# Paired attentions: ScalarE copies both heads' transposes in one instruction, reciprocals for two steps at a time, scores four steps ahead

## The chip, the cores and the metric

The kernel runs on one core of a Trainium2 chip. The metric is the device time of one execution in microseconds (us). The program fills and empties itself within that time: all inputs come from HBM and the result is written back there.

## What is computed

Two networks, one behind the other, on 512 tokens of 1024 features, all in float32. The first has two layers: feed-forward, mixer, feed-forward. The mixer of layer 0 (the "even" one) runs a sparse attention (8 heads in a compressed, a selected and a windowed branch, mixed by gates) beside a dilated attention of 8 heads. The mixer of layer 1 is a multi-head attention with latent projections (MLA) of 16 heads. The second network has a pooling layer and an attention layer with conditioning and convolutional feed-forwards.

```python
def first_block(x, ...):
    for l in range(DEPTH):                      # DEPTH = 2
        x = x + 0.5 * _swiglu(_rms_norm(x, ffn1_norm[l]), ...)
        h = _rms_norm(x, mix_norm[l])
        if l % 2 == 0:
            x = x + _even_mixer(h, ...)
        else:
            x = x + _mla_mixer(h, ...)
        x = x + 0.5 * _swiglu(_rms_norm(x, ffn2_norm[l]), ...)
    return _rms_norm(x, final_norm)

def _probs(scores, mask):
    s = jnp.where(mask, scores.astype(jnp.float32), -MASK_BIG)
    m = jnp.max(s, axis=-1, keepdims=True)
    p = jnp.where(mask, jnp.exp(s - m), 0.0)
    l = jnp.sum(p, axis=-1, keepdims=True)
    l_safe = jnp.where(l > 0, l, 1.0)
    return p / l_safe, (m + jnp.log(l_safe))[..., 0]
```

All that matters here is the causal attention with a softmax: for each head, scores q k^T with a mask, exponentials less the row's maximum, division by the row's sum, and the product with v.

## The kernel before

The kernel is one program written out by engine: each engine has its own instruction stream, and semaphores order them. A weight matrix comes from HBM in tiles (`w_raw`), ScalarE and VectorE split each into a high and a low part (`w_hi`, `w_lo`, lines 1863 and 1883), and TensorE multiplies in three passes (lines 1022 to 1024). That is most of the kernel's time.

The change touches the "paired attention", which is used twice: in the even mixer for 12 pairs of heads (`even_phase`: 8 with gates, being four pairs of heads in two branches, then 4 dilated ones), and in the MLA mixer for 8 pairs. A pair `u` has two heads `a` = 0, 1 and four steps `c` = 0 to 3, one for each block of 128 queries; step `t` = 4u + c. A step with index c covers (c + 1) x 128 keys, since the attention is causal. The eight PSUM banks are used so (`at.bank`): 0 to 3 for scores, two for each parity of t; 4 and 5 for the transposes of head 0 and head 1; 6 and 7 for outputs. One step passes these stations:

- `scores(t)` on TensorE (line 1149): both heads' scores into two banks. In the even mixer three passes (lines 1165, 1167, 1169), in MLA one float32 product (line 1172). It waits until the maxima of t - 2 have freed the banks.
- `maxima(t)` on VectorE (line 2720): adds the mask, writes scores to `wk.sm` in SBUF (shown as scores_even, scores_mla) and takes the row's extreme; one instruction for each head, each followed by a read of the accumulator.
- `exps(t)` on ScalarE (line 2014): exponentials in place, with the row sums in `L`; one for each head.
- `inverse(t)` and `share(t)` on VectorE (lines 2729, 2739, 2741): the reciprocal of both heads' sums, then the scaling of the probabilities, with the gate in the same instruction where there is one.
- `turn_(t)` on TensorE (line 1182): c + 1 transposes of 128 x 128 for each head, head 0 into bank 4, head 1 into bank 5.
- `take(t)`: ScalarE copies head 0's transposes from bank 4 to `wk.pT` (line 2022), VectorE copies head 1's from bank 5 (line 2749). Shown as probs_T_even, probs_T_mla.
- `values(t)` on TensorE (line 1200): the product with v, accumulated in an output bank. After the last step of an output ScalarE and VectorE split the bank into a high and a low part (lines 2032, 2759).

Each engine runs a loop over t with a fixed order. TensorE, after scores 0 to 2: turn_(t), side work, scores(t + 3), values(t - 1). ScalarE, after exps 0 to 2: take(t), exps(t + 3), output, side work. VectorE: take(t), maxima(t + 3), inverse(t + 2), share(t + 2), output, side work. The side work (`beside`, `later`, `added`; lines 1399 to 1402 and 618) exists in the even mixer only: in steps 0 to 5 transposes of values and of compressed probabilities, which ScalarE copies out (lines 1309, 1389, 2078, 2131); splits of queries and keys at steps 5, 8, 11 and so on (lines 1961, 2623); the compressed branch's values after steps 7, 15, 23, 31 (line 1396). Behind the loop follows the output projection (`project_out`, line 1022), whose first weight tiles are loaded and split before it or during it.

## Time and profile before

| | us |
|---|---|
| median of 3 runs | 3224.36 (3220.76 to 3226.31) |
| the profiled execution | 3229.91 |
| its span, first to last instruction | 3228.1 |
| TensorE (PE) busy | 3151.1 (98%) |
| VectorE (DVE) busy | 2001.4 (62%) |
| ScalarE (ACT) busy | 1251.4 (39%) |
| GpSimd (POOL) busy | 179.7 (6%) |
| mean granted TensorE clock | 0.986 of full |

The granted clock is a share of TensorE's upper level, 2.4 GHz; the lower level, 1.2 GHz, is 0.5, and a mean between them is a stretch with both. Busy time of TensorE is partly modelled: the ends of pipelined matmuls overlap the starts of the next, so a stretch in which TensorE waits can look fuller than it is. An instruction's start to the next one's start on the same engine is a better measure of what it costs than its duration, since durations overlap. The chain that ended last is followed back from the end of the program, at each step to what released it.

### The profile page before, as it was taken

Reading aid. Unit: us, or ns where it says so; the run is one execution under the profiler, and the core shown is the slowest. Engines: PE = TensorE matmul, PEld = TensorE weight load, DVE = VectorE, ACT = ScalarE, POOL = GpSimd, SP = SyncE. Lnnn points to the kernel's source line nnn. Section 1 sums busy time; section 2 is a strip of 40 time slices with the busy share of each in tenths; the row PEclk is TensorE's granted clock in tenths of the full one; section 3 lists DMA queues with packets and bytes.
Section 4 is the critical chain, followed back from the end, with each engine's and each line's share of the span. In section 5 each row is a group of like instructions: output and inputs, shape, how many; then the busy total and the mean of one; then the engine's idle time right before and its main releaser. Section 6 shows DMA issues by size and latency. Waiting matters only on the chain.

```text
span 3228.1 us, 43254 instructions
## 1 busy us (share of the span) xinstructions
PE 3151.1 (98%) x15791; PEld 2606.1 (81%) x15791; DVE 2001.4 (62%) x2858; ACT 1251.4 (39%) x1940; POOL 179.7 (6%) x176
## 2 busy tenths in 40 slices
PE   8999999899999999999999999999999999989999
PEld 6888877678888888886688888989888887878887
DVE  6764557966654676457775554997555465565543
ACT  3222423643222422236542233765334343443332
POOL 1000011100000000000020000432000001000000
PEclk9999998999999999999999999999999998999999
DMA  6542342015533455222145433544333230123322
GB/s 182 171 139 100 108 117 65 1 55 165 171 115 100 124 163 149 98 97 66 47 130 172 134 100 109 164 150 144 92 103 98 85 101 4 32 74 91 104 98 72
DMA packets 388600, 346.12 MB, mean 107 GB/s; under 512 B 12512, under 2 KB 340637, under 8 KB 388477
## 3 DMA queue, kind: packets, MB, share of 16 engines
q1 hardware_dynamic: 388477, 344.49, 35.5%
q8 instruction: 76, 1.25, 0.2%
q14 instruction: 47, 0.39, 0.0%
HBM read 338.22 MB, written 2.10 MB: 105 GB/s over the span
## 4 chain that ended last, share of the span: by engine, by line
PE 86%; DVE 9%; ACT 2%; issue 1%; SPq 1%; DMA 0%; POOL 0%; ACTq 0%; DVEq 0%; POOLq 0%
PE ps L1022 26%; PE ps L1023 26%; PE ps L1024 26%; DVE w_lo L1883 2%; PE ps L1112 1%; PE ps L1172 1%; PE ps L1182 1%; PE ps L1200 1%; DVE scores_even L2720 1%; SPq L913 1%; PE ps L1101 1%; ACT scores_even L2014 1%; PE ps L1744 0%; PE ps L1745 0%; PE ps L1743 0%
## 5 line engine op out<-in xcount | busy, mean ns | idle before, releaser
L1022 PE MATMUL ps<-a_hi,w_hi 128*128 128x512 f32 (+1 forms) x2920 | 1105.4, 379 | 31.0 <-DVE t L3249 10.9
L1023 PE MATMUL ps<-a_lo,w_hi 128*128 128x512 f32 (+1 forms) x2920 | 1098.8, 376 | 0.0
L1024 PE MATMUL ps<-a_hi,w_lo 128*128 128x512 f32 (+1 forms) x2920 | 1098.6, 376 | 0.0
L1883 DVE TENSOR_TENSOR w_lo<-w_raw,w_hi 128x1024 fp32r<-128x1024 f32 (+1 forms) x526 | 642.4, 1245 | 173.8 <-ACT w_hi L1863 170.9
L1863 ACT ACTIVATE w_hi<-w_raw 128x1024 fp32r<-128x1024 f32 (+1 forms) x526 | 543.5, 1046 | 353.7 <-PE ps L1024 294.3
L1022 PEld LDWEIGHTS ps<-a_hi,w_hi 128*128 128x128 f32 x2920 | 551.6, 189 | 139.2 <-issue 29.2
L1023 PEld LDWEIGHTS ps<-a_lo,w_hi 128*128 128x128 f32 x2920 | 551.7, 189 | 101.1 <-issue 2.0
L1024 PEld LDWEIGHTS ps<-a_hi,w_lo 128*128 128x128 f32 x2920 | 551.4, 189 | 100.4
L1022 PE MATMUL ps<-hs_hi,w_hi 128*128 128x512 f32 x1008 | 392.7, 390 | 1.0 <-DVE hs_lo L3216 1.0
L1024 PE MATMUL ps<-hs_hi,w_lo 128*128 128x512 f32 x1008 | 392.2, 389 | 0.0
L1023 PE MATMUL ps<-hs_lo,w_hi 128*128 128x512 f32 x1008 | 392.1, 389 | 0.0
L2345 ACT ACTIVATE t<-t 128x512 f32<-128x512 f32 x88 | 55.6, 632 | 518.0 <-DVE t L3193 518.0
L3195 DVE TENSOR_TENSOR t<-ps,rstd 128x512 f32<-128x512 f32 x88 | 60.8, 691 | 294.7 <-PE ps L1024 294.7
L2359 ACT ACTIVATE hs_hi<-hid 128x512 fp32r (+1 forms) x126 | 79.5, 631 | 406.0 <-PE ps L1024 406.0
L1022 PEld LDWEIGHTS ps<-hs_hi,w_hi 128*128 128x128 f32 x1008 | 189.2, 188 | 40.9 <-DVE hs_lo L3216 1.5
L1024 PEld LDWEIGHTS ps<-hs_hi,w_lo 128*128 128x128 f32 x1008 | 189.2, 188 | 39.3
L1023 PEld LDWEIGHTS ps<-hs_lo,w_hi 128*128 128x128 f32 x1008 | 189.2, 188 | 38.9
L3216 DVE TENSOR_TENSOR hs_lo<-hid,hs_hi 128x512 fp32r<-128x512 f32 x106 | 73.3, 691 | 218.3 <-ACT hs_hi L2359 218.3
L3181 DVE SCALAR_TENSOR_TENSOR t<-ps,cols,t 128x511 f32<-128x511 f32 x88 | 66.0, 750 | 188.4 <-ACT t L2338 188.4
L3238 DVE SCALAR_TENSOR_TENSOR ada_acc<-ada_raw,cond,ada_acc 128x1024 f32<-128x1024 f32 x147 | 180.5, 1279 | 0.0
L2338 ACT ACTIVATE t<-ps,cols 128x512 f32<-128x512 f32 x88 | 68.5, 779 | 206.7 <-PE ps L1024 206.7
L3208 DVE TENSOR_TENSOR hid<-t,t 128x512 f32 x108 | 74.8, 693 | 16.9 <-DVE t L3195 8.7
(384 smaller groups left out, 3168.3 us busy)
## 6 DMA issues: line engine op xcount, KB each, us to landing
w_raw<-in_ffn_w_up SPq DMA_DIRECT2D x220, 512.0 KB, 4.7
w_raw<-in_ffn_w_down SPq DMA_DIRECT2D x154, 512.0 KB, 3.5
ada_raw<-in_ada_w SPq DMA_DIRECT2D x96, 512.0 KB, 3.9
w_raw<-in_ffn_w_gate SPq DMA_DIRECT2D x88, 512.0 KB, 5.0
w_raw<-in_ev_w_in SPq DMA_DIRECT2D x20, 512.0 KB, 4.3
w_raw<-in_attn_w_qkv SPq DMA_DIRECT2D x12, 512.0 KB, 3.6
w_raw<-in_mla_w_out SPq DMA_DIRECT2D x8, 512.0 KB, 3.6
w_raw<-in_attn_w_o SPq DMA_DIRECT2D x8, 512.0 KB, 3.6
```

What stands on the lines that cost most here:

```text
L1022: mm(dst, hi, rhi, start=start, stop=False)
L1023: mm(dst, hi, rlo, start=False, stop=False)
L1024: return mm(dst, lo, rhi, start=False, stop=stop)
L1863: nc.scalar.activation(w_hi[:, s, 0:width], w_raw[:, s, 0:width], ACT.Copy).then_inc(hi_made.sem, 1)
L1883: nc.vector.tensor_tensor(w_lo[:, s, 0:width], w_raw[:, s, 0:width], w_hi[:, s, 0:width].bitcast(F32), ALU.subtract).then_inc(lo_made.sem, 1)
L2338: do(t[:, 0:T], ps[:, ph.half + 2 * (f % 2) + side, 0:T], ACT.Identity, scale=conv_column(1, side, f, it), bias=conv_column(3, side, f, it ...
L2359: do(dst, src, ACT.Copy).then_inc(h_hi_s.sem, 1)
L3181: v.scalar_tensor_tensor(t[:, 1:T], src[:, 0:T - 1], conv_column(0, side, f, it), t[:, 1:T], ALU.mult, ALU.add).then_inc(mid.sem, 1)
L3195: v.tensor_tensor(t2[:, 0:T], ps[:, f2 + 1, 0:T], rstd[:, 0:T], ALU.mult).then_inc(up_s.sem, 1)
L3208: v.tensor_tensor(hid[:, bass.ds(it * 2 + f, 1), 0:T], t1[:, 0:T].unsqueeze(1), t2[:, 0:T].unsqueeze(1), ALU.mult).then_inc(h_s.sem, 1)
L3216: v.tensor_tensor(lo, src, hi.bitcast(F32), ALU.subtract).then_inc(h_lo_s.sem, 1)
L3238: last = v.scalar_tensor_tensor(acc, ada_raw[:, u, :], cond[:, c, bass.ds(it, 1)], acc, ALU.mult, ALU.add)
```

## The change

It touches the paired attentions alone.

- The copies. For steps with c = 0, 1 and 2 ScalarE copies both heads' transposes in one instruction, and VectorE has no copy; for c = 3 both copy one head each, as before. Both heads' transposes lie side by side in one bank for c = 0 (bank 4, 256 columns) and c = 1 (bank 5, 512 columns); for c = 2 they lie in banks 4 and 5, and ScalarE's instruction reads 384 columns of each; the new `place(t, a)` says where. ScalarE's copy now waits for both heads' transposes where c < 3.
- TensorE's waits follow from that: `turn_` waits for ScalarE's copy of the step before (c = 0, c = 2 head 1, c = 3), for the one before that (c = 2, head 0), and for VectorE's copy of the last pair's step 3 only at c = 1; `values` waits for VectorE's copy only at c = 3.
- The reciprocals. `inverse(t)` runs for even t only and covers steps t and t + 1 of both heads: four elements a partition. It waits for the exponentials of t + 1.
- The lead. TensorE's scores, ScalarE's exponentials and VectorE's maxima run four steps ahead of the transposes instead of three; ahead of the loop there are four of each. The scaling still runs two ahead.

```diff
--- before.py
+++ after.py
@@ -564,8 +564,14 @@
             n = at.steps = 4 * len(pairs)
             at.tab_in = tab_s.planned
             at.s0, at.sm0, at.p0, at.pn0, at.t0 = s_s.plan(2 * n), sm_s.plan(2 * n), p_s.plan(2 * n), pn_s.plan(2 * n), t_s.plan(2 * n)
-            at.rl0, at.ptd0, at.pta0, at.pv0 = rl_s.plan(n), ptd_s.plan(n), pta_s.plan(n), pv_s.plan(n)
+            at.rl0, at.ptd0, at.pta0, at.pv0 = rl_s.plan(n // 2), ptd_s.plan(n // 4), pta_s.plan(n), pv_s.plan(n)
             at.ph = ph
+
+            def place(t, a):
+
+                c = t % 4
+                return (at.bank(4 + c), a * (c + 1) * P) if c < 2 else (at.bank(4 + a), 0)
+            at.place = place
 
             def bank(x):
 
@@ -1176,10 +1182,13 @@
                     col = (0, 128, 384, 768)[c]
                     for a in range(2):
                         pe.wait_ge(pn_s.sem, at.pn0 + 2 * t + a + 1)
-                        if t:
-                            pe.wait_ge(((pta_s, ptd_s)[a]).sem, (at.pta0, at.ptd0)[a] + t)
+                        bank, at0 = at.place(t, a)
+                        if c == 1 and a == 0 and u:
+                            pe.wait_ge(ptd_s.sem, at.ptd0 + u)
+                        if c == 2 or c != 1 and a == 0 and t:
+                            pe.wait_ge(pta_s.sem, at.pta0 + t - (c == 2 and a == 0))
                         for kb in range(c + 1):
-                            last = nc.tensor.transpose(ps[:, at.bank(4 + a), kb * P:(kb + 1) * P],
+                            last = nc.tensor.transpose(ps[:, bank, at0 + kb * P:at0 + (kb + 1) * P],
                                                        wk.sm[u % 2][:, a, col + kb * P:col + (kb + 1) * P], ident[:, :])
                         last.then_inc(t_s.sem, 1)
 
@@ -1188,7 +1197,8 @@
                     pair = at.heads[u]
                     o = pair["out"]
                     pe.wait_ge(pta_s.sem, at.pta0 + t + 1)
-                    pe.wait_ge(ptd_s.sem, at.ptd0 + t + 1)
+                    if c == 3:
+                        pe.wait_ge(ptd_s.sem, at.ptd0 + u + 1)
                     if c == 0 and pair["first"]:
                         if o >= 2:
                             pe.wait_ge(a_lo_s.sem, at.ph.ol0 + o - 1)
@@ -1202,15 +1212,15 @@
                                       start=kb == 0 and "gate" not in pair, stop=kb == c and "gate" not in pair)
                     last.then_inc(pv_s.sem, 1)
 
-                for t in range(3):
+                for t in range(4):
                     scores(t)
                 for t in range(n + 1):
                     if t < n:
                         turn_(t)
                     if t in beside:
                         beside[t]()
-                    if t + 3 < n:
-                        scores(t + 3)
+                    if t + 4 < n:
+                        scores(t + 4)
                     if t:
                         values(t - 1)
                         if t - 1 in added:
@@ -2015,11 +2025,18 @@
                            accum_out=L[:, u % 2, a, c:c + 1]).then_inc(p_s.sem, 1)
 
                 def take(t):
-                    width = (t % 4 + 1) * P
-                    act.wait_ge(t_s.sem, at.t0 + 2 * t + 1)
+                    c, width = t % 4, (t % 4 + 1) * P
+                    act.wait_ge(t_s.sem, at.t0 + 2 * t + 1 + (c < 3))
                     if t >= 2:
                         act.wait_ge(pv_s.sem, at.pv0 + t - 1)
-                    do(wk.pT[t % 2][:, 0, 0:width], ps[:, at.bank(4), 0:width], ACT.Copy).then_inc(pta_s.sem, 1)
+                    bank = at.place(t, 0)[0]
+                    if c < 2:
+                        do(wk.pT[t % 2][:, :, 0:width], ps[:, bank, 0:2 * width].rearrange("p (a b) -> p a b", a=2), ACT.Copy)\
+                         .then_inc(pta_s.sem, 1)
+                    elif c == 2:
+                        do(wk.pT[t % 2][:, :, 0:width], ps[:, bank:bank + 2, 0:width], ACT.Copy).then_inc(pta_s.sem, 1)
+                    else:
+                        do(wk.pT[t % 2][:, 0, 0:width], ps[:, bank, 0:width], ACT.Copy).then_inc(pta_s.sem, 1)
 
                 def out_hi(t):
 
@@ -2031,12 +2048,12 @@
                         act.wait_ge(cv_s.sem, at.ph.cmp.cv0 + pair["out"] + 1)
                     do(at.ph.o_tile(pair["out"])[0], ps[:, at.bank(6 + pair["out"] % 2), :], ACT.Copy).then_inc(a_hi_s.sem, 1)
 
-                for t in range(3):
+                for t in range(4):
                     exps(t)
                 for t in range(n):
                     take(t)
-                    if t + 3 < n:
-                        exps(t + 3)
+                    if t + 4 < n:
+                        exps(t + 4)
                     out_hi(t - 2)
                     if t in at.later:
                         qk_hi(at.later[t])
@@ -2725,14 +2742,14 @@
 
                 def inverse(t):
                     u, c = divmod(t, 4)
-                    dve.wait_ge(p_s.sem, at.p0 + 2 * t + 2)
-                    v.reciprocal(RL[:, u % 2, :, c], L[:, u % 2, :, c]).then_inc(rl_s.sem, 1)
+                    dve.wait_ge(p_s.sem, at.p0 + 2 * t + 4)
+                    v.reciprocal(RL[:, u % 2, :, c:c + 2], L[:, u % 2, :, c:c + 2]).then_inc(rl_s.sem, 1)
 
                 def share(t):
                     u, c = divmod(t, 4)
                     pair = at.heads[u]
                     col, width = (0, 128, 384, 768)[c], (c + 1) * P
-                    dve.wait_ge(rl_s.sem, at.rl0 + t + 1)
+                    dve.wait_ge(rl_s.sem, at.rl0 + t // 2 + 1)
                     for a in range(2):
                         part, inv = wk.sm[u % 2][:, a, col:col + width], RL[:, u % 2, a, c:c + 1]
                         if "gate" in pair:
@@ -2761,15 +2778,18 @@
                 dve.wait_ge(tab_s.sem, at.tab_in)
                 for t in range(3):
                     maxima(t)
-                    if t:
-                        inverse(t - 1)
-                        share(t - 1)
+                inverse(0)
+                share(0)
+                maxima(3)
+                share(1)
                 for t in range(n):
-                    take(t)
-                    if t + 3 < n:
-                        maxima(t + 3)
+                    if t % 4 == 3:
+                        take(t)
+                    if t + 4 < n:
+                        maxima(t + 4)
                     if t + 2 < n:
-                        inverse(t + 2)
+                        if t % 2 == 0:
+                            inverse(t + 2)
                         share(t + 2)
                     out_lo(t - 2)
                     if t in at.later:
```

## Rows read from the trace of the kernel before

**Rows 1.** The page, part 1: busy us, share of the span, instructions of each engine.

```profile
PE 3151.1 (98%) x15791; PEld 2606.1 (81%) x15791; DVE 2001.4 (62%) x2858; ACT 1251.4 (39%) x1940; POOL 179.7 (6%) x176
```

**Rows 2.** The page, part 4: shares by engine of the chain that ended last.

```profile
PE 86%; DVE 9%; ACT 2%; issue 1%; SPq 1%; DMA 0%; POOL 0%; ACTq 0%; DVEq 0%; POOLq 0%
```

**Rows 3.** Windows, even stage: length; PE, PEld, DVE, ACT, POOL busy; PEclk; DMA; GB/s.

```profile
538.50:567.30 28.80, 22.65 (x132) 15.76 (x131) 21.41 (x72) 13.20 (x42) 0.00 (x0) 0.62 0.00 1
...
577.50:588.90 11.40, 10.24 (x77) 6.46 (x73) 10.83 (x33) 7.04 (x22) 2.15 (x2) 0.85 0.00 0
...
651.40:660.40 9.00, 8.50 (x88) 6.01 (x86) 8.64 (x35) 6.60 (x23) 0.00 (x0) 1.00 0.01 2
```

**Rows 4.** Windows, MLA stage: a pair with and one without a weight split.

```profile
1532.20:1543.20 11.00, 10.38 (x79) 6.64 (x78) 10.45 (x36) 6.68 (x21) 0.00 (x0) 1.00 0.15 49
...
1564.10:1574.00 9.90, 9.90 (x78) 6.65 (x80) 9.35 (x33) 6.69 (x22) 0.00 (x0) 1.00 0.01 2
```

**Rows 5.** The chain in order of time, even stage: start us, us, what.

```profile
636.23 0.85 PE ps L1182 x6
...
642.04 1.02 PE ps L1200 x16
643.07 0.86 PE ps L1396 x4
643.92 0.59 PE ps L1182 x4
...
645.36 0.81 PE ps L1182 x6
...
676.83 0.43 PE ps L1022
```

**Rows 6.** Timeline of TensorE: start us, us, engine, line, tiles, form, count.

```profile
565.44 1.97 PE L1200 MATMUL ps<-probs_T_even,v_tok 128*64 128x128 f32 x16
...
669.34 1.09 PE L1200 MATMUL ps<-probs_T_even,v_tok 128*64 128x128 f32 x16
```

**Rows 7.** Timeline of VectorE in the even stage, 650.6 to 657 us.

```profile
650.66 0.16 DVE L2729 RECIPROCAL pair_stats<-pair_stats 128x2 f32<-128x2 f32 x1
650.86 0.62 DVE L2741 TENSOR_SCALAR scores_even<-scores_even,pair_stats 128x256 f32<-128x256 f32 x2
651.39 0.28 DVE L2749 COPY probs_T_even<-ps 128x128 f32<-128x128 f32 x1
651.59 0.68 DVE L2720 CUSTOM_DVE_ANT_0 scores_even<-ps,masks 128x512 f32<-128x512 f32 x1
...
656.33 0.55 DVE L2749 COPY probs_T_even<-ps 128x384 f32<-128x384 f32 x1
656.80 0.42 DVE L2720 CUSTOM_DVE_ANT_0 scores_even<-ps,masks 128x256 f32<-128x256 f32 x1
```

**Rows 8.** Groups by line and shape, 542 to 683 us: ScalarE's copies (busy us, mean ns).

```profile
L2022 ACT ACTIVATE probs_T_even<-ps 128x512 f32<-128x512 f32 x12 | 6.9, 577 | 1.0 <-PE ps L1182 1.0
...
L2022 ACT ACTIVATE probs_T_even<-ps 128x384 f32<-128x384 f32 x12 | 5.7, 475 | 0.7 <-PE ps L1182 0.7
...
L2022 ACT ACTIVATE probs_T_even<-ps 128x256 f32<-128x256 f32 x12 | 4.4, 365 | 0.0
...
L2022 ACT ACTIVATE probs_T_even<-ps 128x128 f32<-128x128 f32 x12 | 3.1, 255 | 0.0
```

**Rows 9.** The chain in order of time, MLA stage.

```profile
1506.33 4.23 PE ps L1172 x12
...
1528.12 1.29 PE ps L1172 x4
...
1533.96 1.13 DVE w_lo L1883
...
1590.73 0.43 PE ps L1022
```

**Rows 10.** Groups by line and shape, 542 to 683 us: idle before the transposes.

```profile
L1182 PE MATMUL ps<-ident,scores_even 128*128 128x128 f32 x240 | 42.1, 302 | 10.8 <-ACT probs_T_even L2022 6.2 <-DVE probs_T_even L2749 3.7 <-DVE scores_even L2739 0.8
```

## The prediction

> **What bounds the kernel now.** I read the busy shares first, then the chain of work that ended last, then stretches of time around the two paired attentions. TensorE is busy 98% of the span and carries 86% of the chain [rows 1, 2]: over the whole kernel it is the bound, so time given back anywhere else counts only where TensorE waits. The change touches two stretches. The first is the attention of the even block, 12 pairs of heads, from 538.5 us to 676.83, where the output projection's first matmul runs [rows 3, 5]: 138.3 us. The second is the MLA attention, 8 pairs, from 1506.33 to 1590.73 [rows 9]: 84.4 us. Together 222.7 us of 3228.1. Outside them nothing changes, and the projections behind them are chained matmuls, so a stage that ends sooner moves everything behind it.
>
> In these stretches the reader is to see two engines that are both nearly full. In a later even pair (651.4 to 660.4) VectorE is busy 8.64 of 9.00 us, ScalarE 6.60 [rows 3]. TensorE shows 8.50, but its ends are modelled; the chain gives its real need. From 636.23 to 645.36 the chain is TensorE without a gap: 9.13 us for four steps with one extra group, the compressed values of 0.86, so 8.27 us a pair [rows 5]. Pairs 8 to 10 take 642.04 to 669.34, from the last group of values of pair 7 to that of pair 10: 27.3 us, 9.1 each [rows 5, 6]. So there VectorE holds TensorE back by 0.8 a pair. Pairs 1 to 7 (565.44 to 642.04) take 76.6 us, 10.94 each [rows 5, 6]; VectorE is busy 10.83 of 11.40 in one of these stretches, at a granted clock of 0.85, that is, partly at 1.2 instead of 2.4 GHz [rows 3]. In MLA it is the other way round: a regular pair takes 9.90 us in which TensorE is busy 9.90 and VectorE 9.35; TensorE is the bound. But two pairs of eight take 11.0, as in 1532.2 to 1543.2, where a weight split of 1.13 us stands before VectorE's copy in the chain [rows 4, 9].
>
> **Part by part.** (1) VectorE loses the copies of steps with c = 0, 1, 2. From start to start the one of 128 columns takes 651.39 to 651.59 and the one of 384 takes 656.33 to 656.80; the one of 256 I put halfway: 0.20 + 0.33 + 0.47 = 1.00 us a pair [rows 7]. (2) It loses two of four reciprocals a pair; one takes 650.66 to 650.86, 0.20; the one that stays has four elements instead of two a partition, which I cost at nothing: 0.40 a pair [rows 7]. Sum: 1.40 us a pair on VectorE, 28 us over 20 pairs. It is not a gain of 28: what it gives is set by TensorE's need.
>
> (3) ScalarE's copies widen. They last 255, 365, 475 and 577 ns for 128, 256, 384 and 512 columns, about 107 ns for 128 more [rows 8]. After: 365 (c=0), 577 (c=1), 768 columns over two banks (c=2, no such row: 577 + 2 x 107 = 791), 577 (c=3, unchanged). 2.31 instead of 1.67, so +0.64 us a pair. ScalarE is busy 6.60 of 9.00; 7.3 still fits, so it hides. The bounds of the c=2 copy are 791 and, if two banks cost as two instructions, 2 x 475 = 950; I take 791, the slope of four rows. The Trainium skill (ScalarE: Activation LUTs, What ACT_TABLE_LOAD costs) gives 186 ns + 0.833 ns an element, 826 ns for this copy; by it ScalarE would have 0.04 us more a pair, and the sum would not move.
>
> (4) New waits. ScalarE's copy now waits for both heads' transposes; queued behind it are the exponentials of four steps on, the output copy and splits, and for it wait the values of the step and, for c = 3, the next transposes. VectorE's reciprocal waits for the exponentials of one step more; behind it stand the scaling of the probabilities, and TensorE's transposes wait for those. Between that step's maxima and the reciprocal VectorE still has a scaling and the next maxima to do, while ScalarE's copy and exponentials run: I cost it at nothing, at worst a few tenths a time. TensorE loses its wait for VectorE's copy in three of four steps; the profile shows 3.7 us of such waits and 6.2 us for ScalarE's copy in the even stage [rows 10]. The lead of four steps moves no semaphore closer by itself: scores of t+4 still wait for maxima of t+2, two iterations old, as before. No DMA and no queue of SyncE or GpSimd is moved.
>
> (5) The sum by place, before minus after.
> - Even pairs 1 to 7: VectorE gives 7 x 1.40 = 9.8. TensorE's need is 7 x 8.27 = 57.9, four groups of compressed values at 0.86 (3.4), about 2.2 for the zero matmuls and one side transpose, and about 3.5 lost to the lower clock (an estimate: the granted clock is 0.85 in one stretch of 11.4 us, where 0.15 of it is given up, and similarly in its neighbours): 67.0. So at most 9.6 of 76.6. With both engines then near 9.5 a pair they can't interleave perfectly; I take three quarters, 7.2. Bounds: 0 and 13 (if the clock stays up as well).
> - Even pairs 8 to 10: floor 3 x 8.27 = 24.8 of 27.3, 2.5; I take 2.1. The last pair, 669.34 to 676.83, drains: 0.4.
> - Even pair 0, 538.5 to 565.44, 26.9 us at a granted clock of 0.62 [rows 3, 6]. It is a serial loop through scores, maxima, exponentials, a side copy on ScalarE and side transposes, and the loop stays. The prologue is longer by one score step, and the first transposes wait for exponentials of step 1 and stand behind the maxima of step 2 (about 1 us later), but one step more is done by then. VectorE's removed work helps in three loops. I take 1.0, bounds -1 and 3.
> - MLA: the two pairs of 11.0 fall to 9.9, 2.2; start and drain 0.7. In all 2.9, bounds 1 and 5.2 (84.4 less 8 x 9.90).
>
> 7.2 + 2.1 + 0.4 + 1.0 + 2.9 = 13.6 us. The profiled execution took 3229.91, so 3216.3 for one like it; the median of the runs is 3224.36, so 3210.8. I go by the median.
>
> **The rivals.**
> (A) TensorE reaches its floor everywhere and the clock stays up: 13 + 2.5 + 0.5 + 3 + 5.2 = 24.2, giving 3200.2. For it: 9.90 of 9.90 in MLA shows the engines can interleave perfectly. Against: even pairs carry splits, output copies and GpSimd work at uneven places.
> (B) Latency, not VectorE's throughput, sets the even pairs: a step goes through maxima, exponentials, scaling, transposes and copy, and the change shortens none of these but the copy on VectorE. Then pairs 1 to 7 give 1 or 2 us, the rest a little, MLA 2: about 5 us, 3219.4. For it: ScalarE's exponentials are in the chain, and its busy share is low. Against: VectorE's 95%.
> (C) Slower: ScalarE's copy becomes the link TensorE waits for. It starts only when head two is transposed, half a group of transposes later (the groups take 0.59, 0.81 and, for c = 3, 1.02 in the chain [rows 5]; by the same steps 0.37 for c = 0; so 0.19 + 0.30 + 0.40 = 0.89 a pair), and lasts 0.64 longer, all of it in front of the c = 3 transposes. If all 1.53 lie on the path, MLA loses 8 x 1.53 = 12.2 less the 2.9, and the even pairs 12 x 0.13 = 1.6: 10.9, 3235.3. It decides once the copy of c = 2 ends later than TensorE is through with the scores and values that it runs in between: in MLA 1.29 of scores and 0.59 of values (a group of eight, taken like its four transposes), 1.9 us [rows 5, 9]; in the even stage the groups of transposes and of values take 0.37 + 0.59 + 0.81 + 1.02 = 2.79 each, which leaves 2.7 of 8.27 for four groups of scores and 0.7 for this one, 1.3 us in all. Against it stand 0.79 and a handoff, provided that ScalarE is free. That last condition speaks for it: ScalarE must first finish the exponentials of step t+3, which start only after the maxima. By the trace two maxima and two exponentials follow one another with little between, so in the even stage this is close; in MLA the longer scores leave 0.6 us more.
> (D) A copy is much dearer on ScalarE. VectorE's copies of 128 and 384 columns last 0.28 and 0.55 [rows 7], so 0.42, 0.69, 0.96 and 0.69 for the four new widths, 2.76; three times that is 8.3. ScalarE's other work is 6.60 less 1.67, 4.9, so 13.2 a pair against a mean of 11.1 now (222.7 over 20): 20 x 2.1 = 42, 3266. Against it: 384 columns take 475 ns on ScalarE and 550 on VectorE [rows 7, 8]. The Trainium skill (Trainium Architecture — The Big Picture, Inside one NeuronCore) says of simple arithmetic that VectorE is up to about three times as fast for each element, which would speak against moving copies; for copies out of PSUM the trace disagrees.
>
> **Chances.** Forecast 0.61, A 0.12, B 0.16, C 0.10, D 0.01. A change of 0.2% is 6.4 us, about what can be told from none. The forecast lies beyond that, its lower tail (some 0.04) doesn't: faster 0.61 - 0.04 + 0.12 + 0.06 of B = 0.75; slower 0.08 (most of C, and D); same 0.17. The range 3201 to 3221 holds the forecast with its bounds, most of A and B, and leaves out C, D and the end of A.
>
> **What would show it.** VectorE: 24 fewer copies in the MLA stage and 36 in the even one, 40 reciprocals instead of 80. ScalarE's c = 2 copy near 791 ns. Even pairs 1 to 7 at about 9.9 us, pairs 8 to 10 at 8.4, MLA pairs all at 9.9. TensorE's waits for VectorE's copies gone, those for ScalarE's copies not grown. The forecast is wrong if ScalarE's copies head the waits before the c = 3 transposes (C), if VectorE shows gaps while even pairs stay above 10.5 (B), or if the first pair grows by several us.

## The result and the profile after

| | before | changed |
|---|---|---|
| median, us | 3223.46 (6 runs, 3220.76 to 3226.31) | 3210.91 (6 runs, 3209.83 to 3213.09) |
| the profiled execution, us | 3229.91 | 3210.06 |
| its span, us | 3228.1 | 3208.3 |
| mean granted clock | 0.986 | 0.993 |

The ratio is 0.9961, with a 95% interval of 0.995 to 0.9971: 12.5 us less. The two profiled executions differ by 19.9 us, 7 more than the medians; the profile of before, at 3229.91, is a high one of its kernel. What part of the extra lies in untouched code, and what part in a lower clock within the two stretches, is told below.

The page's part 1 of the changed kernel answers rows 1, and its part 4 rows 2:

```profile
PE 3129.6 (98%) x15791; PEld 2591.2 (81%) x15791; DVE 1976.2 (62%) x2758; ACT 1263.3 (39%) x1940; POOL 180.5 (6%) x176
...
PE 86%; DVE 8%; ACT 2%; issue 1%; SPq 1%; DMA 0%; POOL 0%; ACTq 0%; DVEq 0%; POOLq 0%
```

VectorE has 100 instructions fewer (60 copies, 40 reciprocals), ScalarE as many as before. Over the span the shares have hardly moved, as they could not: what counts are two stretches of it. Windows of the even stage, against rows 3 (length; PE, PEld, DVE, ACT, POOL busy; clock; DMA share; GB/s): pair 0, pair 2, pairs 9 and 10, then pairs 1 to 7 in one window.

```profile
538.20:562.50 24.30, 16.37 (x126) 11.49 (x125) 19.23 (x63) 14.43 (x43) 0.00 (x0) 0.86 0.00 1
...
573.70:583.70 10.00, 9.59 (x93) 6.42 (x91) 9.11 (x30) 7.89 (x25) 2.49 (x2) 1.00 0.00 0
...
641.80:650.50 8.70, 8.27 (x88) 6.00 (x86) 7.53 (x29) 7.20 (x22) 0.00 (x0) 1.00 0.00 1
650.50:658.70 8.20, 7.76 (x82) 5.58 (x80) 7.03 (x26) 6.71 (x20) 0.00 (x0) 1.00 0.01 2
```

```profile
562.50:632.20 69.70, 64.69 (x609) 44.78 (x607) 60.19 (x200) 52.38 (x151) 9.03 (x8) 0.98 0.01 1
```

The same window of the kernel before, pairs 1 to 7:

```profile
565.40:642.00 76.60, 68.48 (x611) 47.16 (x609) 69.94 (x235) 49.10 (x153) 8.57 (x8) 0.93 0.01 1
```

The reader is to see two things. First, VectorE's busy time in pairs 1 to 7 fell from 69.94 to 60.19 us: 9.75, or 1.39 a pair, and ScalarE took 3.3 us more. About 1.1 of the 9.75 are neither copies nor reciprocals: the gated scalings of 384 columns took less time, of which the last section says more (before, then changed):

```profile
L2739 DVE TENSOR_SCALAR scores_even<-scores_even,pair_stats,gates 128x384 f32<-128x384 f32 x14 | 9.0, 687 | 0.3
...
L2756 DVE TENSOR_SCALAR scores_even<-scores_even,pair_stats,gates 128x384 f32<-128x384 f32 x14 | 7.9, 602 | 0.3
```

Without them it is 1.24 a pair, as it is in pairs 8 to 10; over the whole span VectorE's busy time fell by 25.2 us, 1.26 for each of the 20 pairs.

Second, the mean granted clock of this stretch rose from 0.93 to 0.98, and so the stretch shortened for two reasons. Pair 1 is at 0.84 before and 0.85 after. Pairs 2 and 3, however, were at 0.86 and 0.85 before (first two lines) and at 1.00 in the changed kernel (pair 2 stands above, pair 3 is the third line):

```profile
576.44:588.85 12.41, 11.25 (x91) 7.47 (x89) 11.89 (x36) 7.70 (x25) 2.15 (x2) 0.86 0.00 0
588.85:600.02 11.17, 9.94 (x86) 7.06 (x84) 9.53 (x34) 6.69 (x21) 0.00 (x0) 0.85 0.01 2
...
583.67:592.96 9.29, 8.53 (x87) 5.98 (x85) 7.67 (x26) 7.01 (x21) 0.00 (x0) 1.00 0.01 3
```

In the kernel before TensorE was busy 21.19 us in pairs 2 and 3, and 18.18 in pairs 4 and 5, which do the same work at 1.00. So some 3.0 us of the shortening may be the clock (an estimate). Pairs 4 to 7 are at 1.00 in both kernels and compare cleanly: 41.95 us before and 39.26 after, 0.67 a pair. Seven times that is 4.7.

By place, each from the first matmul of a group to that of the next (before, rows 5, 6 and 9), the changed kernel in its profile, and in a second profile of the same kernel (e10, below):

| | before | changed | again |
|---|---|---|---|
| even pair 0 | 26.9 (clock 0.62) | 24.1 (0.86) | 25.9 (0.71) |
| even pairs 1 to 7 | 76.5 | 69.8 | 70.3 |
| of these, pairs 4 to 7 (clock 1.00 in all three) | 41.95 | 39.26 | 39.26 |
| even pairs 8 to 10 | 27.4 | 26.5 | 26.5 |
| even pair 11 | 7.4 | 6.9 | 6.9 |
| MLA, up to the last values of pair 0 | 16.0 (0.90) | 14.7 (1.00) | 17.7 (0.81) |
| MLA, from there to the projection | 68.3 | 65.9 | 65.9 |

The chain of the changed kernel in MLA, against rows 4 and 9: from the second half of pair 0 on it is TensorE alone, but for one ScalarE copy of 0.82 us in the last pair, and each pair takes 9.90, the two that had 11.0 too.

```profile
1501.11 0.70 PE ps L1191 x4
...
1510.10 1.02 PE ps L1210 x16
...
1520.00 1.03 PE ps L1210 x16
...
1529.90 1.02 PE ps L1210 x16
...
1539.80 1.03 PE ps L1210 x16
...
1575.99 0.43 PE ps L1028
```

### The profile page after: what moved, and what is told of

Read it like the earlier page. It is cut to its first block, busy times and chain, and to the rows that moved or that the text cites. A ratio compares the mean times of both kernels' runs of the same rounds, so it can differ in the third digit from the quotient of the medians.

```text
span 3208.3 us, 42990 instructions
## 1 busy us (share of the span) xinstructions
PE 3129.6 (98%) x15791; PEld 2591.2 (81%) x15791; DVE 1976.2 (62%) x2758; ACT 1263.3 (39%) x1940; POOL 180.5 (6%) x176
## 4 chain that ended last, share of the span: by engine, by line
PE 86%; DVE 8%; ACT 2%; issue 1%; SPq 1%; DMA 0%; POOL 0%; ACTq 0%; DVEq 0%; POOLq 0%
PE ps L1028 26%; PE ps L1030 26%; PE ps L1029 26%; DVE w_lo L1893 2%; PE ps L1118 1%; PE ps L1191 1%; PE ps L1210 1%; PE ps L1178 1%; ACT scores_even L2024 1%; SPq L919 1%; PE ps L1107 1%; DVE scores_even L2737 1%; PE ps L1754 0%; PE ps L1755 0%; PE ps L1753 0%
```

## The experiments

The variants differ from the kernel before or from the changed kernel in these stages only. Their times stand beside runs of the kernel before on the same chip; the stages are read from each variant's profile, as in the table above.

**e1, the merged copies alone.** The kernel before with `place`, its waits and ScalarE's merged copy:

```diff
+            at.place = place
 ...
+                    if c < 2:
+                        do(wk.pT[t % 2][:, :, 0:width], ps[:, bank, 0:2 * width]..., ACT.Copy)
 ...
-                    take(t)
+                    if t % 4 == 3:
+                        take(t)
```

> The kernel before with the merged copies alone: lead three, one reciprocal a step. Theory (VectorE's load sets the even pairs, TensorE's need the floor): VectorE loses 1.00 of the 1.40 us a pair, so even pairs 1 to 7 fall from 76.6 us to about 71.5, MLA pairs all to 9.9, and the time is about 9 us under the kernel before, 3214. Rival (the lead and the paired reciprocals bring the gain, because they take ScalarE's exponentials out of VectorE's way): within 3 us of the kernel before, and the copies of c = 2 are in front of most transposes of c = 3.

Measured: 3218.82 (11 runs) beside 3224.44, ratio 0.9983 (0.9974 to 0.9992), 5.6 us. Even stage 132.7 us in place of 138.2, MLA 82.1 in place of 84.3; pairs 1 to 7 71.8. Two MLA pairs still take 10.6. The load theory expected 71.5 for pairs 1 to 7, but the clock is at 0.99 there against 0.93 before; in pairs 4 to 7, at 1.00 in both, the gain is 1.4 us (40.55 for 41.95), 0.35 a pair for 1.00 off VectorE. The total was expected too high; the copy of c = 2 did come to stand in front of the transposes, as the rival said: TensorE's waits from 565 to 660 us were

```profile
PE ps L1191 <- ACT probs_T_even L2037: 5.4, 8, 1.4
PE ps L1191 <- DVE scores_even L2756: 1.4, 4, 0.5
PE ps L1191 <- ACT probs_T_even L2034: 1.2, 3, 0.5
```

**e5, the paired reciprocals and the lead alone.** The kernel before with

```diff
-                    if t + 3 < n:
-                        scores(t + 3)
+                    if t + 4 < n:
+                        scores(t + 4)
 ...
-                    v.reciprocal(RL[:, u % 2, :, c], L[:, u % 2, :, c])
+                    v.reciprocal(RL[:, u % 2, :, c:c + 2], L[:, u % 2, :, c:c + 2])
```

> The kernel before with paired reciprocals and the lead of four alone; each engine copies one head, as before. Theory (load): VectorE loses 0.40 us a pair, 12 x 0.4 = 5 in the even stage of which TensorE sees 3, MLA 1: 3219 to 3220. Rival (lead): most of the change's 12.5 us, under 3214.

Measured: 3222.10 (11 runs) beside 3224.44, ratio 0.9993 (0.9984 to 1.0002), 2.3 us and within the interval of nothing. Even 135.1, MLA 81.6. Without the merged copies the lead does not bring most of the gain, so the rival fails in this form. The two halves give 5.6 and 2.3, together 8 of 12.5: the change is worth more than its parts. Which part needs which, e2 and e3 show.

**e2, one reciprocal a step.** The changed kernel with

```diff
-                    dve.wait_ge(p_s.sem, at.p0 + 2 * t + 4)
-                    v.reciprocal(RL[:, u % 2, :, c:c + 2], L[:, u % 2, :, c:c + 2]).then_inc(rl_s.sem, 1)
+                    dve.wait_ge(p_s.sem, at.p0 + 2 * t + 2)
+                    v.reciprocal(RL[:, u % 2, :, c], L[:, u % 2, :, c]).then_inc(rl_s.sem, 1)
```

> The changed kernel with one reciprocal a step again, copies merged and lead four kept. Theory (load): 0.40 us a pair comes back on VectorE, of which the even pairs 1 to 7 show about 2: 3213, 2 us over the changed kernel, and MLA, where TensorE is at its floor, shows nothing. Rival (the pairing matters by its waits): since it waits for fewer exponentials it is as fast as the changed kernel or faster, 3210.

Measured: 3212.98 (5 runs) beside 3224.44, ratio 0.9963 (0.995 to 0.9977), beside the change's 0.9961 (0.995 to 0.9971): by time the two can't be told apart. Nor do the places show a price. Pairs 8 to 10 take 26.5 us and MLA 80.8, as in the changed kernel. Pairs 1 to 7 take 72.1, 1.8 to 2.4 more, which looks like the 2 that were expected; but all of it lies in pair 4, and there the granted clock fell to 0.87 (e2, then the changed kernel):

```profile
595.27:608.07 12.80, 11.28 (x92) 7.40 (x90) 11.30 (x37) 8.51 (x25) 2.15 (x2) 0.87 0.01 2
...
592.96:603.33 10.37, 9.55 (x91) 6.40 (x89) 9.95 (x34) 8.28 (x24) 2.36 (x2) 1.00 0.01 2
```

The other pairs at 1.00 take the same in both: pairs 2 and 3 together 19.3 us, pairs 5 to 7 28.89. So 0.40 us a pair on VectorE more or less changes nothing here, and the agreement with the expectation was luck. Whether the fall of the clock in pair 4 has to do with the single reciprocals, one profile can't show.

e2 shows something else by what it differs from e1 in, which is the lead alone: merged copies and single reciprocals in both, a lead of three in e1 and of four in e2. The slowest of e2's five runs took 3214.75, the fastest of e1's eleven, on the same chip, 3216.31; the medians are 5.8 us apart. So with the merged copies the lead of four is worth about as much as the copies themselves (5.6). By place, MLA behind pair 0 falls from 67.6 to 65.9, where TensorE's waits for the copy of c = 2 fall from 1.6 to 0.4 us; in the even stage its waits for the copies of c = 0 and 1 (line 2034), 1.7 us in e1, are gone.

**e3, a lead of three.** The changed kernel with `t + 3` for `t + 4` on the three engines.

> The changed kernel with a lead of three for scores, maxima and exponentials, paired reciprocals and merged copies kept. Theory: the reciprocal then waits in each second step for exponentials whose maxima VectorE has only just finished, 1.2 to 1.8 us for 512 columns and about 1 for 256; of two such waits a pair the even stage shows nearly all (12 x 2.2 = 26 us) and MLA what exceeds VectorE's slack of about 2 us a pair (8 x 0.5 = 4): 3240. Rival: the lead is of no account, 3211.

Measured: 3240.23 (5 runs) beside 3224.44, ratio 1.0048 (1.0034 to 1.0061): 15.8 us slower than before. Even 144.9, MLA 91.1. VectorE's longest waits from 568.5 to 675 us, and a stretch of its timeline in MLA:

```profile
DVE pair_stats L2746 <- ACT scores_even L2024: 17.9, 20, 1.0
```

```profile
1554.31 0.08 DVE L2737 DVE_READ_ACCUMULATOR2_ANT pair_stats<- 128x1 f32 x1
1555.27 0.18 DVE L2746 RECIPROCAL pair_stats<-pair_stats 128x4 f32<-128x4 f32 x1 [0.88 <-ACT scores_mla L2024]
...
1559.34 0.08 DVE L2737 DVE_READ_ACCUMULATOR2_ANT pair_stats<- 128x1 f32 x1
1560.18 0.18 DVE L2746 RECIPROCAL pair_stats<-pair_stats 128x4 f32<-128x4 f32 x1 [0.76 <-ACT scores_mla L2024]
```

Twice a pair the reciprocal stands 0.8 to 0.9 us idle until ScalarE has the exponentials of the step whose maxima VectorE has just finished. In the changed kernel one such wait of 0.4 us is left in each stage. I had put the even stage's loss at 26 us and it was 17.6 against the changed kernel: the waits are shorter than I took. MLA's I had put at 4 and it was 10.5; of these, 4.5 lie before the last values of pair 0, at a granted clock of 0.73 against 1.00, and 6.0 behind them.

With merged copies throughout, the medians (us) of the four kernels are these; three of them stand beside 3224.44 for the kernel before, and that of the change beside 3223.46:

| | one reciprocal a step | paired reciprocals |
|---|---|---|
| lead of three | 3218.82 (e1) | 3240.23 (e3) |
| lead of four | 3212.98 (e2) | 3210.91 (the change) |

At a lead of three the paired reciprocals cost 21.4 us. At a lead of four they cost nothing, and gain nothing that can be told from none.

**e4, VectorE relieved, ScalarE not loaded.** The kernel before with

```diff
+                    width = 16 if t >= 4 and t % 4 < 3 else width
                     v.tensor_copy(wk.pT[t % 2][:, 1, 0:width], ps[:, at.bank(5), 0:width]).then_inc(ptd_s.sem, 1)
```

> The kernel before, but from step 4 on VectorE's copies with c = 0, 1, 2 take only 16 columns, so the rest of head two's probabilities is not copied: part of the result is left out. It relieves VectorE of about 0.7 us a pair and loads ScalarE with nothing. If VectorE's load is all that counts, it gives less than the merged copies alone (which took 1.00 off and gave 5.5 us in the even stage and 2.3 in MLA): about 4 and 1.8. If the merged copy also costs time, because ScalarE starts it only after both heads' transposes and takes longer, it gives as much or more: 6 or over in the even stage.

Measured: 3216.33 (10 runs) beside 3223.26, ratio 0.9978 (0.9969 to 0.9987), 6.9 us; the interval overlaps e1's, so the times don't decide. Even 131.0 (7.2 less), MLA 81.5 (2.9 less), but the even stage has a pair 0 of 24.9 at a clock of 0.76 in it, where e1 had 26.7 at 0.63. By the other places: in pairs 1 to 7 e4 takes 72.8 and e1 71.8, 3.7 and 4.7 less than before, part of it by the clock (1.00 and 0.99 for 0.93). In pairs 4 to 7, at 1.00 in all, they give 1.1 and 1.4 us, in the order of what they take off VectorE (estimated at 0.7 and 1.0 a pair). In pairs 8 to 10 it is 26.1 against 26.8, and in MLA behind pair 0 66.7 against 67.6: there the one that relieves less gives more. So VectorE's copy was in the way in pairs 1 to 7, and where TensorE is nearly full the merged copy has a price of its own, the later start and the longer copy on ScalarE. Whether it was in the way by its load or as a link that TensorE waited for isn't separated, since e4 shortens that link too.

**e9, the price of the copy of c = 2.** The changed kernel with

```diff
                     elif c == 2:
+                        width = 16 if t >= 4 else width
                         do(wk.pT[t % 2][:, :, 0:width], ps[:, bank:bank + 2, 0:width], ACT.Copy).then_inc(pta_s.sem, 1)
```

> The changed kernel, but from step 4 on ScalarE's copy with c = 2 takes 16 columns of each head instead of 384, so part of the probabilities is not copied: about 0.6 us a pair less on ScalarE, all of it in front of the transposes of c = 3. Theory (ScalarE's c = 2 copy has become the link in the even pairs): pairs 8 to 10 fall from 8.8 us to about 8.4, and the even stage loses 4 to 6 us; MLA, at TensorE's floor, nothing but its drain. Rival (VectorE is still the link): the even stage stays within 1.5 us.

Measured: 3210.15 (4 runs) beside 3223.26, ratio 0.9959 (0.9944 to 0.9974). Pairs 8 to 10 fell from 26.5 to 25.3, 8.4 each, as the theory has it. But pairs 1 to 7 took 71.0, against 69.8 and 70.3 in the changed kernel. Pairs 2 and 4 are 0.75 and 0.57 us longer than there, at a clock of 1.00, and VectorE is busy 10.28 and 10.49 us in them for 9.09 and 9.95: the gated scalings of 384 columns fell beside GpSimd's work more often (9.2 us in all for 7.9). So the shorter copy moved another delay into the way. The expectation of 4 to 6 us in the even stage was a miss, and what the copy of c = 2 costs in pairs 1 to 7 stays open.

**e6 and e8, ScalarE's side work first.** The chain of the changed kernel from one group of transposes to the next, in pair 9, shows what stands there:

```profile
644.50 0.37 ACT scores_even L2024
644.92 0.68 ACT scores_even L2024 x3
645.60 0.48 ACT F_r L2049
646.08 0.70 ACT probs_T_even L2037
646.92 1.06 PE ps L1191 x8
```

The output's copy (line 2049) runs between the exponentials and the copy of c = 2 (line 2037), for which TensorE's eight transposes wait. e6 moves ScalarE's side copies of steps 0 to 5 ahead of the exponentials; e8 moves the splits and the output copy too, this one a step later:

```diff
                     take(t)
+                    if t in beside:
+                        beside[t]()
+                    out_hi(t - 3)
+                    if t in at.later:
+                        qk_hi(at.later[t])
                     if t + 4 < n:
                         exps(t + 4)
-                    out_hi(t - 2)
-                    if t in at.later:
-                        qk_hi(at.later[t])
-                    if t in beside:
-                        beside[t]()
```

> The changed kernel with ScalarE's side copies (steps 0 to 5 of the even stage) ahead of the exponentials of the same iteration. Theory (pair 0 is a serial loop in which TensorE's side transposes wait for a copy that stands behind exponentials, which wait for maxima, which wait for TensorE): four or five loops lose some 1 us each, pair 0 falls from 24.1 us to about 20, and the time is 3207. Rival (VectorE's softmax of the compressed branch sets pair 0): pair 0 stays within 1 us, 3210.

> The changed kernel with all of ScalarE's side work ahead of the exponentials: side copies, the splits of queries and keys, and the copy of the output, which moves one step later (as does VectorE's half of it). Theory: the splits and output copies no longer stand before the copy of c = 2, and VectorE no longer waits for ScalarE's half of a split (4.4 us in all): besides pair 0's 4 us, pairs 1 to 10 lose about 0.3 each, 3204. Rival (exponentials delayed by 0.5 us hold up the reciprocals instead): pairs 1 to 7 grow, 3210 or more.

Measured: e6 3206.19 (5 runs), ratio 0.9955 (0.9941 to 0.9968); e8 3200.37 (5 runs), ratio 0.9931 (0.9917 to 0.9944), both beside 3223.26. e6's interval overlaps the change's, so its gain is shown by the place and not by the time. Pair 0 takes 19.7 us in both. Pairs 1 to 7: 69.7 in e6, 65.5 in e8; pairs 8 to 10: 26.5 and 25.0. e8's interval lies wholly below that of the change: the best version of the study, 22.9 us under the kernel before. Its chain in pairs 8 and 9 is TensorE alone: the group of eight transposes begins as soon as the values before it are done, and the pair takes 8.22, against 8.27 worked out from rows 5.

```profile
632.82 1.02 PE ps L1210 x16
...
636.88 0.59 PE ps L1210 x8
637.47 1.02 PE ps L1191 x8
638.50 0.43 PE ps L1171 x2
...
641.04 1.02 PE ps L1210 x16
```

**e10 and e7.** The changed kernel again, and beside it one with only the output's copy moved (`out_hi(t - 3)` ahead of the exponentials, `out_lo(t - 3)`).

> The changed kernel once more, unaltered, beside e7 on one chip. What is open is pair 0 of the even stage: it took 24.1 us at a granted clock of 0.86 in the changed kernel's profile, 26.9 at 0.62 before, and 26.7, 25.4, 25.9 and 26.6 at 0.63, 0.69, 0.70 and 0.64 in four variants. If the change shortens pair 0, it is near 24 here whatever the clock; if it was the clock's draw, pair 0 takes 25 to 27 with the clock at 0.6 to 0.7. Pairs 1 to 7 near 70 us and MLA at 80.6 either way, the time 3211.

> The changed kernel with only the output's copy out of PSUM moved: ScalarE's half one step later and ahead of the exponentials, VectorE's half one step later. Theory (it is this copy that stands before the copy of c = 2 in the pairs that end an output): pairs 8 to 10 fall from 26.4 us to about 25.2, pairs 1 to 7, with an output in three of seven, lose 1 to 2, pair 0 stays: 3208. Rival (the splits of queries and keys brought all of it): pairs 8 to 10 stay at 26.4.

Measured, beside 3222.97: e10 3211.50 (5 runs), ratio 0.9962 (0.9948 to 0.9976); e7 3209.70 (4 runs), ratio 0.9957 (0.994 to 0.9973). In e10 pair 0 takes 25.9 us at a clock of about 0.7, so most of what the first profile showed there went with the clock. MLA takes 83.6 and not the 80.6 expected, all of the difference before the last values of pair 0, at a clock of 0.81. e7's interval overlaps e10's, so here too only the places speak. In e7 pairs 8 to 10 take 25.1 and pairs 1 to 7 68.9: for the last pairs the output's copy is the whole of it, and in pairs 1 to 7 the splits bring the larger part (68.9 to 65.5 in e8; from pair 2 on, at a clock of 1.00 in all, 58.5 in the changed kernel, 57.8 in e7 and 54.5 in e8).

## Why the prediction was right

Predicted were 3210.8 us and a gain of 13.6; measured are 3210.91 and 12.5. That the time agrees to 0.1 us is luck: the sum was taken from 3224.36, and the median of before came out at 3223.46. The total is right, but the runs divide it otherwise than the prediction did. Its step (4) put the lead of four at nothing (it "moves no semaphore closer by itself"), and its step (2) counted the paired reciprocals as 0.40 us a pair of relief. Measured beside the merged copies, the lead brings 5.8 us (e1 to e2), and the paired reciprocals nothing that can be told from none (e2 to the change). By steps:

- **VectorE loses 1.40 us a pair.** Nearly so: 1.24 to 1.26; the 1.39 in pairs 1 to 7 has the shorter scalings in it. The reciprocal of four elements costs 9 ns more than that of two, where I took nothing, and ScalarE's copy of 768 columns takes 792 ns where the slope gave 791 (tile views below). The estimate of 826 ns from the rate in the Trainium skill (ScalarE: Activation LUTs, What ACT_TABLE_LOAD costs) is 4% high; the trace decides, and the sum doesn't move. ScalarE's busy time grew by 11.9 us over the span, 0.60 a pair, where 0.64 was worked out.
- **Pairs 1 to 7, 7.2.** Measured 6.8 and, in the second profile, 6.2, both against one profile of before in which pairs 2 and 3 ran at a lower clock. The sum had left the clock as it was, so this agreement is partly luck: what pairs 4 to 7 show at one clock comes to 4.7 for seven pairs, and the term was about half too large. Nor do three quarters of VectorE's relief show as time: at 1.00, e4, e1, e5 and the change give 1.1, 1.4, 0.6 and 2.7 us in pairs 4 to 7, a little under half of what they take off VectorE (2.8, 4.0, 1.6 and 5.6, estimated as in the prediction), and e2, with 0.40 a pair more on VectorE, loses nothing in the pairs at 1.00. "They can't interleave perfectly" was right for this order of the work, not in principle: e8 gets 65.5, under the floor of 67.0 that I had. That floor had 3.5 for the clock, which is at 1.00 from pair 1 on in e8, and a fourth group of compressed values, which belongs to the next stretch [rows 5].
- **Pairs 8 to 10, 2.1.** Measured 0.9. This term was mis-sized: I took TensorE's floor for what comes next, and it was ScalarE's copy behind the output's copy, rival C's mechanism at a quarter of its price. e9, e7 and e8 each take 1.2 to 1.4 us out there. The floor itself, 24.8, left out the compressed group of 0.86 that stands at 643.07 [rows 5]; but the longer lead also moves the last step's scores ahead of this stretch, and TensorE alone takes 25.0 there in e8.
- **Pair 0, 1.0.** Measured 2.8 and 1.0 in two profiles of one kernel, at different clocks. The variants that keep this loop take 25.4 at a clock of 0.69 (e2), 25.4 at 0.69 (e7), 25.9 at 0.70 (e5), 26.7 at 0.63 (e1) and 26.6 at 0.64 (e9). A gain of 1 can't be shown or excluded.
- **The last even pair 0.4 and MLA 2.9.** Measured 0.5, and 2.4 behind pair 0 of MLA; the start of MLA took 16.0 before, and 14.7 and 17.7 in two profiles of the changed kernel, with the granted clock at 0.90, 1.00 and 0.81.
- On the side of the changed kernel these terms repeat: 6.5 (the mean of two) + 0.9 + 0.5 + 2.4 = 10.3 us. With 4.7 for pairs 1 to 7 at one clock it would be 8.5. The rest of 12.5 lies in pair 0, MLA's start and the clock, in an amount that single profiles don't fix.

One sign of being wrong did appear, that ScalarE's copies head the waits before the transposes of c = 3. In the even stage of the changed kernel TensorE's waits before its transposes are these (line 2037 is the copy of c = 2):

```profile
PE ps L1191 <- ACT probs_T_even L2037: 5.3, 9, 0.9
...
PE ps L1191 <- DVE scores_even L2756: 1.2, 3, 0.5
```

Before it was 6.2 for ScalarE's copies and 3.7 for VectorE's [rows 10]. So C's link is there, but it replaces two others that together were longer, and the kernel became faster.

The rivals: A (the floor everywhere) was not reached by the change. e8's 3200.37 is A's 3200.2 only in the total, since 7.2 of e8's gain lie in pair 0, where A had 3. B would have given 5 us, with 1 or 2 in pairs 1 to 7, where 6.2 to 6.8 were measured, and about 4.7 at one clock. It isn't wholly out: pairs 1 and 6 stay above 10.5 us (11.2 and 10.9) with VectorE busy 8.0 and 8.9, e4 can't tell it from load, since it shortens the copy too, and the gain by the lead comes without any load taken off. C exists at 0.4 us a pair in pairs 8 to 10 and does not decide; D is refuted by the 792 ns.

Between the two profiles the two stretches differ by 14.7 us; the rest of the 19.9 lies in code that no edit touches. From the MLA projection to the end the kernel before took 1637.4 us and the changed one 1632.3; between the stages 829.6 and 829.7. In windows of 60 us at the same places of the program the granted clock is below 1.00 in five before and in four after, and the sum of what is missing is 0.34 against 0.21, that is, full clock for 20 and 13 us in all not granted. The two windows with the largest difference are these; in one between them it is the other way round, 0.99 before and 0.94 after (length, TensorE busy, clock, DMA share, GB/s). That the clock makes all of the 5.1 us is what is left, and isn't shown. The windows, before and then changed:

```profile
2670.70:2730.70 60.00, 56.00 (x321) 0.86 0.00 1
2850.70:2910.70 60.00, 52.78 (x223) 0.90 0.25 72
```

```profile
2656.00:2716.00 60.00, 55.07 (x355) 0.94 0.00 1
2836.00:2896.00 60.00, 57.35 (x244) 0.94 0.31 88
```

## What to carry to other kernels

Where two engines are near full in a stage, what an edit takes off the one is only a bound on the gain: here a little under half of it was seen at best, and of the paired reciprocals' share nothing. Compare stretches at the same granted clock before dividing a gain among causes. Then look for what stands in line before the next link on the third engine, since that is where the rest of the gain stays. In a software pipeline let an in-order engine do its independent side work before the instruction that will have to wait, not after it: that reordering gave another 10 us in this kernel, nearly as much as the change itself. And a step that makes an instruction wait for one iteration more (the paired reciprocal) needs one iteration more of lead: with it the wait was free, without it the kernel was 16 us slower than before. Test such a pair of edits in all four combinations: here the lead, from which nothing had been expected, was worth 5.8 us by itself beside the merged copies, and the reciprocals nothing that shows.

## What the runs showed of the hardware

- ScalarE reads two PSUM banks in one instruction with no extra cost: 792 ns for 2 x 384 columns, where 512 in one bank take 576 and the slope of the one-bank copies gives 791. VectorE's reciprocal of four elements a partition takes 173 ns, of two 164. From the tile views of the changed kernel, and for the two elements of the kernel before (columns: line, engine, operation, tiles, count, then min/median/max ns, first and last start, form).

```profile
L2037 ACT ACTIVATE probs_T_even<-ps x12: 785/792/811, 551.2 to 661.7; 128x768 f32<-128x768 f32 x12
L2039 ACT ACTIVATE probs_T_even<-ps x12: 573/576/597, 555.9 to 663.3; 128x512 f32<-128x512 f32 x12
```

```profile
L2746 DVE RECIPROCAL pair_stats<-pair_stats x40: 169/173/181, 543.4 to 1569.6; 128x4 f32<-128x4 f32 x40
...
L2729 DVE RECIPROCAL pair_stats<-pair_stats x80: 156/164/171, 542.3 to 1585.9; 128x2 f32<-128x2 f32 x80
```

- VectorE's scaling of the probabilities takes longer beside GpSimd's work. Two instructions of 128 x 384 with gates take 0.87 us alone, and 1.59 when GpSimd's masking of the compressed probabilities starts beside them (VectorE's and GpSimd's timelines of the changed kernel). The Trainium skill (SBUF — State Buffer, SBUF: two separate sides) says that VectorE in a two-port mode and GpSimd lock one pair of ports against each other for whole instructions; the longer time agrees with that, but no view shows the mode, and no run here takes GpSimd's work away. That it lengthens the pairs isn't shown either, except in e9, where pairs 2 and 4 grew with it.

```profile
586.23 0.87 DVE L2756 TENSOR_SCALAR scores_even<-scores_even,pair_stats,gates 128x384 f32<-128x384 f32 x2
...
594.87 1.59 DVE L2756 TENSOR_SCALAR scores_even<-scores_even,pair_stats,gates 128x384 f32<-128x384 f32 x2
```

```profile
595.00 2.36 POOL L3544 TENSOR_TENSOR cmp_pd<-cmp_pT,cmp_own 128x512 f32<-128x512 f32 x2 [16.78 <-PE ps L1406]
```

- In pair 0 of the even stage, where TensorE waits much, the granted clock of the same kernel was 0.86 in one execution and 0.71 in another, and the stretch took 24.1 and 25.9 us. At other places too it differed between kernels that do the same work there: 0.86 and 1.00 in pair 2 (before, changed), 1.00 and 0.87 in pair 4 (changed, e2). A gain of 1 or 2 us in such a place can't be read from single profiles.
